# Compression products of the pages with 512 columns moving, in quarters of the weights

## What is computed

```
def phi(rows, pe, w1, w2):
    blk = rows[:, idx] + pe[None, None, :, None, :]
    flat = jnp.moveaxis(blk, 3, 2).reshape(b, n_cmp, g, CMP_LEN * hd)
    return jax.nn.silu(flat @ w1) @ w2
...
kc = rope(phi(k_raw, pe_k, wk1, wk2), end)
vc = phi(v_raw, pe_v, wv1, wv2)
```

## Time and profile before

| what | value |
|---|---|
| median of 3 runs | 927.91 us |
| the profiled execution's own time | 928.51 us |
| its span | 926.8 us |
| PE busy | 904.8 us, 98% of the span |
| DVE busy | 647.7 us, 70% |
| ACT busy | 453.4 us, 49% |
| POOL busy | 189.2 us, 20% |
| mean granted TensorE clock | 0.997 |

### The profile page before, as it was taken

How to read it: one execution, slowest core, us unless ns; L and a number is a source line. 1 busy time by engine, 2 the same in 40 slices (tenths; PEclk the granted TensorE clock), 3 DMA queues, 4 the chain that set the end, 5 groups by cost and what they waited for, 6 DMA issues and landing times.

```text
span 926.8 us, 21926 instructions
## 1 busy us (share of the span) xinstructions
PE 904.8 (98%) x8176; PEld 846.9 (91%) x8176; DVE 647.7 (70%) x1447; ACT 453.4 (49%) x896; POOL 189.2 (20%) x321
## 2 busy tenths in 40 slices
PE   6999999999999999999999999999999999999997
PEld 6999899988888799999999998999888878999996
DVE  6999767677666467656769996666766565775574
ACT  6444655564543454344543447654554444443352
POOL 1200000237658300000000000003574771000000
PEclk9999999999999999999999999999999999999998
DMA  9762985736979874333665577666469799335421
GB/s 327 290 225 104 423 335 205 271 118 217 306 224 299 255 319 161 138 138 120 256 254 206 196 301 267 257 271 271 165 194 301 239 272 332 159 140 196 165 92 51
DMA packets 66345, 209.89 MB, mean 226 GB/s; under 512 B 12192, under 2 KB 49776, under 8 KB 56256
## 3 DMA queue, kind: packets, MB, share of 16 engines
q1 hardware_dynamic: 57200, 187.67, 55.3%
q0 software_dynamic: 8896, 20.82, 7.1%
q10 hardware_dynamic: 144, 0.01, 0.0%
HBM read 202.48 MB, written 41.36 MB: 263 GB/s over the span
## 4 chain that ended last, share of the span: by engine, by line
PE 86%; SPq 4%; DMA 3%; ACT 2%; DVE 2%; issue 2%; DVEq 0%; ACTq 0%
PE bank L1027 63%; PE bank L1275 7%; PE bank L1040 4%; SPq L851 4%; PE bank L1195 2%; DMA paged<-in_pool 2%; PE bank L1165 1%; PE bank L1157 1%; PE bank L1309 1%; ACT paged_r L1540 1%; DMA x<-in_x 1%; PE bank L1405 1%; PE bank L1208 1%; PE bank L1377 1%; ACT kvp L1508 0%
## 5 line engine op out<-in xcount | busy, mean ns | idle before, releaser
L1782 DVE TENSOR_TENSOR big_r<-big,paged_r 128x1024 fp32r<-128x1024 f32 (+1 forms) x160 | 194.6, 1221 | 74.0 <-ACT paged_r L1540 73.1
L1027 PE MATMUL bank<-xnT_high_r,paged_r 128*128 128x288 f32 x768 | 231.7, 302 | 0.0
L1027 PE MATMUL bank<-xnT_r,paged_r 128*128 128x288 f32 x704 | 207.6, 295 | 0.0
L1027 PE MATMUL bank<-xnT_high_r,big_r 128*128 128x288 f32 x704 | 207.1, 294 | 0.0
L1540 ACT ACTIVATE paged_r<-big 128x1024 fp32r<-128x1024 f32 (+1 forms) x160 | 166.7, 1049 | 4.3 <-DMA big<-in_w_feat 2.4
L1027 PE MATMUL bank<-short_r,big_r 128*128 128x288 f32 x568 | 167.5, 295 | 0.0
L1027 PEld LDWEIGHTS bank<-xnT_high_r,paged_r 128*128 128x128 f32 x768 | 144.0, 188 | 5.1 <-issue 2.7
L1027 PEld LDWEIGHTS bank<-xnT_high_r,big_r 128*128 128x128 f32 x704 | 132.4, 188 | 0.0
L1027 PEld LDWEIGHTS bank<-xnT_r,paged_r 128*128 128x128 f32 x704 | 132.2, 188 | 0.0
L1027 PE MATMUL bank<-short_r,paged_r 128*128 128x288 f32 x440 | 130.9, 298 | 1.2 <-DVE big_r L1782 1.1
L1027 PE MATMUL bank<-kvp_r,paged_r 128*128 128x288 f32 x440 | 130.4, 296 | 0.0
(11 more groups left out here) (347 smaller groups left out, 1818.9 us busy)
## 6 DMA issues: line engine op xcount, KB each, us to landing
big<-in_w_tok SPq DMA_DIRECT2D x13, 2048.0 KB, 9.9
big<-in_w_feat SPq DMA_DIRECT2D x12, 2048.0 KB, 8.2
big<-in_w_gate SPq DMA_DIRECT2D x10, 2048.0 KB, 9.6
out_kept_dil<-in_cache_dil SPq DMA_DIRECT2D x16, 1020.0 KB, 13.2
paged<-in_pool SPq DMA_DIRECT2D x218, 64.0 KB, 4.5
big<-in_w_up SPq DMA_DIRECT2D x12, 1024.0 KB, 8.9
paged<-in_pool POOLq DMA_DIRECT2D x166, 64.0 KB, 5.1
big<-in_kv_win SPq DMA_DIRECT2D x4, 2048.0 KB, 8.8
```

The lines of the kernel that those rows point to most:

```text
L1027: last = mm(out, l, r, start=(c == 0 and i == 0), stop=(c == n - 1 and i == 2))
L1782: v.tensor_tensor(l_part[:, rest], full[:, rest], h_part[:, rest].bitcast(FP32), ALU.subtract)\
```

## The change

A piece now holds all 32 pages of a group and a quarter of the weights (`q` 0 to 3): 2 parts by 2 slices by 3 products, 12 matmuls with 512 columns moving. Part 1 comes first and part 0 second, and each part's sum fills a bank of its own, from the first piece of the group to the fourth. `hpost` and `htail` come once for a group, over 512 columns. Rounding and splitting take 1024 columns for each piece as before, but all four requests' pages of the group must be there before its first piece is rounded, and no page's place is free before its fourth piece is done. `vc`, `imp` and both `impsum` move from the ring `PJ` to `TR`. `vc` 0 and `kc` 1 stand one place later in the list, and some small steps stand behind `hpost` instead of ahead of it. The selected keys and values are placed anew: the values of half 0 go into halves of `long` and `x`, those of half 1 into `paged[0]`. `x` is loaded back for the end of the layer once those values have been used.

```diff
-    pieces = [(hb, kind, bp, lh) for hb in range(HB) for kind in range(2) for bp in range(2) for lh in range(2)]
+    pieces = [(hb, kind, q) for hb in range(HB) for kind in range(2) for q in range(4)]
...
-           [("sgateA", 0), ("sscore", 1, "d4")] + piece(("cmpt", 0), ("sscore", 1, "mix"), ("sturn", 0, "win")) + \
+           [("sgateA", 0), ("sscore", 1, "d4")] + piece() + [("cmpt", 0), ("sscore", 1, "mix"), ("sturn", 0, "win")] + \
            [("sexp", 1, "A")] + piece() + \
-           [("vc", 0), ("spv", 0, "win"), ("sturn", 1, "d4")] + piece() + \
-           [("spv", 1, "d4"), ("sturn", 1, "mix"), ("imp", 0)] + piece() + \
-           [("impsum", 0), ("spv", 1, "mix"), ("sturn", 1, "anew")] + \
-           piece(("spv", 1, "anew"), ("soA", 1)) + piece() + [("kc", 1)] + \
-           piece(("sgateA", 1), ("sscore", 1, "win")) + piece() + \
+           [("spv", 0, "win"), ("sturn", 1, "d4")] + piece() + \
+           [("vc", 0), ("spv", 1, "d4"), ("sturn", 1, "mix"), ("imp", 0)] + piece() + \
+           [("impsum", 0), ("spv", 1, "mix"), ("sturn", 1, "anew")] + piece() + \
+           [("spv", 1, "anew"), ("soA", 1)] + piece() + \
+           piece(("sgateA", 1), ("kc", 1), ("sscore", 1, "win")) + piece() + \
            [("sscore", 1, "cmp"), ("sexp", 1, "cmp"), ("sscore", 0, "slc0"), ("sscore", 0, "slc1"), ("sexp", 0, "slc")] + piece()
-    out += [("cmpt", 1), ("sturn", 0, "cnew"), ("sscore", 1, "new"), ("hpost", 1, 1, 1), ("htail", 1, 1, 1), ("sturn", 0, "slc0"), ("sexp", 1, "win"),
+    out += [("cmpt", 1), ("sturn", 0, "cnew"), ("sscore", 1, "new"), ("hpost", 1, 1), ("htail", 1, 1), ("sturn", 0, "slc0"), ("sexp", 1, "win"),
             ("imp", 1), ("spv", 0, "cnew"), ("sturn", 0, "slc1"), ("vc", 1), ("impsum", 1)] + splits(("gate", 0, 0), 0) + \
...
-    in_turn_bank = lambda s: s[0] == "kc" or s == ("impsum", 0)
+    in_turn_bank = lambda s: s[0] in ("kc", "vc", "imp", "impsum")
...
+        if k in ("proj", "gc", "feat", "gkc", "gate", "up", "down"):
             pj_keys.append((layer, s))
...
+        if k == "hid" and s[3] == 0:
+            pj_keys += [(layer, ("sums",) + s[1:3] + (part,)) for part in (1, 0)]
...
-    PAGE_PLACES = [paged[0], paged[1], big[0], long]
-    PAGE_SLOTS = {("cmp", 0, 0): 1, ("cmp", 1, 0): 0, ("cmp", 0, 1): 1, ("cmp", 1, 1): 0, ("slc", 0, 1): 2,
-                  ("slc", 0, 0): 1, ("slc", 1, 0): 0, ("slc", 1, 1): 3}
+        both("slc", 0, 0) + both("slc", 1, 0) + both("slc", 1, 1)
+    PAGE_PLACES = [paged[0][:, 0:2048], paged[0][:, 2048:4096], paged[1][:, 0:2048], paged[1][:, 2048:4096],
+                   big[0][:, 0:2048], big[0][:, 2048:4096], long[:, 0:2048],
+                   x[:, :, :].rearrange("p k n -> p (k n)")[:, 0:2048]]
+    PAGE_SLOTS = {("cmp", 0, 0): 2, ("cmp", 1, 0): 0, ("cmp", 0, 1): 2, ("cmp", 1, 1): 0, ("slc", 0, 1): 4,
+                  ("slc", 0, 0): 2, ("slc", 1, 0): 6, ("slc", 1, 1): 0}
+    page_slot = lambda key: PAGE_SLOTS[key[0:3]] + key[3]
...
         kind, which, hb, h = key
         if kind == "cmp":
-            return PJ.is_full(("hid", hb, which, h), layer)
+            return PJ.is_full(("sums", hb, which, 0), layer)
...
         elif key[0:3] == ("slc", 0, 1):
             queue.wait_ge(*big_used(Now.layer, ("kA", 1)))
-        elif key[0:3] == ("slc", 1, 1):
-            queue.wait_ge(*PJ.is_full(("hid", 1, h, 1)))
+        elif key[0:3] == ("slc", 1, 0):
+            queue.wait_ge(*PJ.is_full(("sums", 1, 0, 0)))
         else:
             queue.wait_ge(*pages_used(*PG[z].before(key)))
         for i in page_share(key, z):
...
                 elif k == "hid":
-                    _, hb, kind, bp, lh = s
-                    key = s[0:4]
-                    if lh == 0:
-                        wait(pe, PJ.is_free(key))
+                    _, hb, kind, q = s
                     for part in range(2):
                         pe.wait_ge(*w1_split.at((kind, part)))
                     pe.wait_ge(*pages_split.at(s[1:]))
                     ph, pl = page_parts(s[1:])
-                    for j in range(4):
-                        for part in (1, 0):
-                            at = P * (4 * lh + j)
+                    for part in (1, 0):
+                        key = ("sums", hb, kind, part)
+                        if q == 0:
+                            wait(pe, PJ.is_free(key))
+                        out = pj(key)[:, :].rearrange("p (m n) -> p m n", m=RB * PAGES)
+                        for j in range(2):
+                            at = P * (2 * q + j)
                             wh = W1_HIGH[kind][part][:, at:at + P]
                             wl = w1_low[:, 2048 * kind + 1024 * part + at:2048 * kind + 1024 * part + at + P]
-                            out = pj(key)[:, 256 * (1 - part):256 * (2 - part)].rearrange("p (m n) -> p m n", m=16)
                             for n, (w, r) in enumerate(((wh, ph), (wh, pl), (wl, ph))):
-                                last = mm(out, w, r[:, :, j, :], start=(lh == 0 and j == 0 and part == 1 and n == 0),
-                                          stop=(lh == 1 and j == 3 and n == 2), skip_group_check=True)
-                    last.then_inc(*(PJ.fill(key) if lh else half_done.inc(s[1:])))
+                                last = mm(out, w, r[:, :, j, :], start=(q == 0 and j == 0 and n == 0),
+                                          stop=(q == 3 and j == 1 and n == 2))
+                        if q == 3:
+                            last.then_inc(*PJ.fill(key))
+                    if q < 3:
+                        last.then_inc(*quarter_done.inc(s[1:]))
...
-                    wait(pe, PJ.is_free(s))
-                    mm(pj(s)[:, 0:NBLK + 1], PTc[hb][:, :], overlap[:, :], start=True, stop=True)\
-                        .then_inc(*PJ.fill(s))
...
                 elif k == "pround":
                     n = PIECES.index(s[1:])
-                    hb, kind, bp, lh = s[1:]
+                    hb, kind, q = s[1:]
                     for pg in PG:
-                        act.wait_ge(*pg.is_full(("cmp", kind, hb, bp)))
+                        for h in range(2):
+                            act.wait_ge(*pg.is_full(("cmp", kind, hb, h)))
...
                         before = PIECES[n - 2]
-                        act.wait_ge(*(PJ.is_full(("hid",) + before[0:3]) if before[3] else half_done.at(before)))
```

On VectorE the change to `hpost` (`htail` becomes one operation of 512 columns):

```diff
                 elif k == "hpost":
-                    _, hb, kind, bp = s
-                    key = ("hid",) + s[1:]
-                    if (hb, kind, bp) == (0, 0, 0):
+                    _, hb, kind = s
+                    first, second = (("sums", hb, kind, part) for part in range(2))
+                    if (hb, kind) == (0, 0):
                         dve.wait_ge(*unit_used(UNITS[-1]))
-                    dve.wait_ge(*hid_done.at(HIDDEN[HIDDEN.index(key) - 1]))
-                    dve.wait_ge(*PJ.is_full(key))
+                    dve.wait_ge(*hid_done.at(HIDDEN[HIDDEN.index(("hid", hb, kind)) - 1]))
+                    dve.wait_ge(*PJ.is_full(second))
                     by_head = lambda z: z.rearrange("p (m g i) -> p g m i", g=KV, i=8)
                     in_heads = lambda z: z.rearrange("p (g m i) -> p g m i", g=KV, i=8)
-                    link(v.tensor_copy(in_heads(old[:, 1279:1535]), by_head(pj(key)[:, 0:256])))
+                    v.tensor_copy(in_heads(hidt_next), by_head(pj(second)[:, :])).then_inc(*PJ.release(second))
+                    dve.wait_ge(*PJ.is_used(second))
+                    dve.wait_ge(*PJ.is_full(first))
                     for g in range(KV):
-                        last = v.scalar_tensor_tensor(in_heads(hidp)[:, g, :, :], by_head(pj(key)[:, 256:512])[:, g, :, :],
+                        last = v.scalar_tensor_tensor(in_heads(hidp)[:, g, :, :], by_head(pj(first)[:, :])[:, g, :, :],
                                                       pe_b[:, kind:kind + 1], in_heads(hidt)[:, g, :, :], ALU.add, ALU.add)
-                    last.then_inc(*PJ.release(key))
+                    last.then_inc(*PJ.release(first))
```

110 lines of the change are left out of this document (54 added, 56 removed).

## The result

The changed kernel takes 943.09 us, the median of 5 runs (939.25 to 947.22), against 927.95 us for the kernel before on the same chip: the ratio is 1.0158 [1.0133, 1.0182]. It is 15 us slower where 3.3 us were forecast, and above the range of 925 to 937 us. The profiled execution is the longest of the five, 947.22 us with a span of 945.5 us and a mean granted clock of 0.982 (0.997 before; the other four have 0.984 to 0.987). It is 18.7 us over the profiled execution of before; the medians differ by 15.1 us.

The account below looks back on a forecast made before the run. PE was taken as the bound, SP's page queue very close. Per layer +0.2 (keys), -0.2 (piece 15), +2.0 (behind it), -0.5/-0.2 (values): +3.3 us on 928.51, 931.8, less 0.6 for the median: 931.2 us; range 925 to 937 us.

Parts of the forecast that it names:

- pages behind piece 7: 17 pages issued in a row on SP in 8.90 us; window load at 276.0 us, against 276.18 us before.
- the chain behind piece 15: Wider DVE and ACT operations and the bank shared by `vc` and `imp` delay the first gate product: +2.0 us a layer.
- The start of the scores: First scores against selected keys: PE waits for late pages, +0.2 us a layer, bounds -3.2 and +1.6 us.
- from the window load on nothing is changed: SP's queue in layer 0: 34 pages and 4.26 us of landing as before, keys there at 300.5 us.
- Rival (b): Wider product saves nothing (243.6 ns), the 17 pages behind piece 7 take 10.42 us: 938.0 us; chance 0.25 with its half form.
- The wide product: In all 32 pieces, one 512-column matmul takes 226 ns: 0.21 us less a piece, 6.7 us in all.
- what is left over does not grow: Compression products: time beyond the columns stays at 12.7 ns for 512 columns, as in the 288-column row.
- The rounding of piece 8: ACT waits 1.5 us for both page halves; piece 8 starts near 269.7 us against 270.49; PE loses under 1 us.
- its sign: Behind piece 15, `vc` would wait more than 1 us for DVE's copy of `imp`.
- Selected values: Half 0's values are issued ahead of piece 15, so PE's waits of 0.5 and 0.2 us go.

Follow-up runs that it names:

- late_last: Kernel before, with only the page group of pieces 4 to 7 kept whole until piece 7 is done; 937.40 us, ratio 1.0089.
- swap_after: Changed kernel with selected keys exchanged: half 0 loaded ahead of half 1, into the large buffer free early; 939.30 us, ratio 1.0109.
- swap_gate: Changed kernel with selected keys exchanged and the second half of half 0's selected values issued behind the first gate weights; 935.57 us, ratio 1.0076.
- fill: Changed kernel with dummy products of 512 columns, 20 and 12, in PE's two longest waits of each layer; 941.31 us, ratio 1.0137.
- 930.9 (banks): Changed kernel with keys exchanged, half the selected values behind the gate weights, and half 1's `vc`, `imp`, `impsum` in the projections' banks; 930.94 us, ratio 1.0022.

## Why the prediction was wrong

The place was right: pages behind piece 7, then the chain behind piece 15. Two terms of the sum failed. The start of the scores was put at +0.2 us a layer and is +2.7 and +4.0; the step behind it is that from the window load on nothing is changed, and that the products save 1.7 us by then. From there to the gate product +1.8 us a layer was taken (2.0 less 0.2 for piece 15) and it is +6.6 and +5.0; there the sum has no term for the clock. Rival (b) is the nearest: the products save almost nothing. But its slow pages were another group than it said, and its 938.0 us were still 5 us short. Step by step:

- **The wide product.** Taken as 226 ns, it is 239.0. What failed is that "what is left over does not grow", read from rows of 256 and 288 columns. But the 288-column rows are of another product (L1027) and read other operands, and nothing in them tells how a product in runs of 16 scales. What is left over is 25.7 ns, 1.7 times the 15.1 of the earlier trace rows. It saves 4.6 ns in place of 17.6 a pair: 1.8 us in all, not 6.7. Piece 7 ends 0.46 us sooner (35.20 for 35.66 us), where 1.7 was taken. The Trainium skill (TensorE: Matmul & The Clock Gate, Back-to-back issue gap) would have 2.5 ns left over. The trace disagrees even for one run of columns, 17 ns over at 512. The same section calls this the gap of a single matmul and gives about 131 ns at 512 columns for a stream of weight loads and matmuls, which lies further still from the 239.0 ns here.
- **The pages.** "I put the start at +0.2 us against before": it is +2.7 and +4.0 us. Counted from piece 0, the window load in layer 0 is 1.85 us later than before, 2.0 later than taken: 1.2 from the product, and 0.7 because the 17 pages took 9.60 us and not 8.90. In layer 1 they took 8.56 us and it is 0.8 us later than before. "From there nothing is changed" failed too, in layer 1 above all: from the window load to the scores it is 25.5 and 27.4 us, 24.6 and 24.2 before, with 12.68 and 14.16 us for the first 17 pages where the prediction had 10.42. One premise was a misreading: the run of 8.90 us was called undisturbed, and a large load the reason for the 10.42 us. But the 8.90 us run stands right behind a large load as well: SP issues `big<-in_v_a` (L944, 1792 KB) at 684.88 us and these pages from 685.41 us on. One part held: that the group of pieces 4 to 7 decides, as the prediction said, late_last shows.
- **The rounding of piece 8.** Covered, as taken, in the changed kernel's layer 0. In layer 1 ACT stood idle 2.50 us before it, and piece 8 starts 1.0 us later than before where 0.8 sooner was taken; with the keys in time it starts 1.9 and 2.2 us later there (swap_after, swap_gate).
- **Behind piece 15.** +1.8 us a layer was taken, piece 15 included, and with the clock held up it is +2.3 (fill): the size was near. DVE's copy of `imp` starts 4.16 us behind its copy for the last sum, said to be 4.2. The distance from that copy to the gate product, said to be 8.7 us, is 10.9 (313.87 to 324.74 us): `vc` and the scores of half 1 take 1.94 and 3.63 us at 1.2 GHz. `vc` did wait 1.02 us for the copy of `imp`, as its sign said. A wait not foreseen is that for ACT's copies, 1.45 us: the prediction asked who shares a bank with `imp` and not how it moves the ring's turn for the transposes.
- **Selected values.** The waits of 0.5 and 0.2 us went. But the same move set nine pages ahead of the gate weights; the prediction named who waits for these values and not who stands behind them in the queue. No wait of PE shows it as long as the keys were later still; once they were not it cost 3.7 us in medians (swap_after against swap_gate), with overlapping intervals.
- **The term that is missing.** No sum had the clock in it. A wait was priced at its length. In the profiled execution of late_last, waits of 4.9 and 2.7 us took 2.4 and 1.6 us more behind them, in products at 1.2 GHz; in that of the changed kernel it is 4.4 and 2.6 us, the largest single share of what the sum lacks. In medians the share is smaller and open.

In us of the median, the repairs went 943.1, 939.3 (keys), 935.6 (gate weights), 930.9 (banks); the shares depend on the order, as the banks show, which gave nothing ahead of the gate weights. The last is on the chip where before takes 928.4: 2.5 us are left. In its trace, from the start of piece 15 to the gate product it is 2.9 us (layer 0) and 1.0 us (layer 1) longer than before; piece 15 itself starts 2.0 us sooner in layer 0, and in layer 1, behind a late piece 8, 0.7 us later. Which operation behind piece 15 makes it no run took apart.

## What to carry to other kernels

When an edit makes a buffer come free later, go through the queue load by load, not only to the first user that waits: the order in which loads of different urgency share it decided here, and exchanging two groups took away 7.5 of the 10 us that the late release cost. A wait of PE can cost its length and what runs at the lower clock behind it; put both in the sum. A step that takes its turn in a ring of banks moves the turn of all that follow it. And the cost of a product at another size is taken only from a row with the same pattern of access: where there is none, the sum should be made at the worse end, too.
